# Result transposes one score later, narrow scores in turns with value products, and a later wait for the low weights, in a sparse-attention and SSM trunk

## What is computed

```python
def compressed_attention(q, kc, vc, scale): ...   # softmax over 63 compressed keys
def selected_attention(q, ks, vs, idx, scale): ... # top-16 of 16 blocks: all causal keys
def window_attention(q, kw, vw, scale):            # causal, the last 512 keys
    ...
        sc = jnp.einsum('bghtd,bsgd->bghts', qi, kk) * scale
        p = jax.nn.softmax(jnp.where(valid, sc, MASK_VALUE), axis=-1)
        return jnp.einsum('bghts,bsgd->bghtd', p, vv)
o_attn = g3[..., 0:1] * o_cmp + g3[..., 1:2] * o_slc + g3[..., 2:3] * o_win
```

## Time and profile before

| | |
|---|---|
| median of 3 executions | 937.76 us (937.34 to 938.78) |
| the profiled execution | 937.52 us |
| its span | 935.7 us |
| mean granted TensorE clock | 0.999 |
| PE busy | 896.5 us (96%) |
| VectorE, ScalarE, GpSimd busy | 520.3, 394.9, 215.0 us |
| chain that ended last, by engine | PE 88%, ACT 4%, DVE 3%, DMA 2% |

### The profile page before, as it was taken

One profiled execution on the slowest core, in us unless ns is written; L12 is line 12 of the kernel. 1 busy time (PEld: TensorE's weight loads), 2 busy tenths in 40 slices (PEclk: granted clock), 3 DMA queues, 4 the chain that ended last, 5 costly groups with the idle time before them and its releaser, 6 DMA issues.

```text
span 935.7 us, 14442 instructions
## 1 busy us (share of the span) xinstructions
PE 896.5 (96%) x5585; PEld 739.4 (79%) x5593; DVE 520.3 (56%) x1090; ACT 394.9 (42%) x793; POOL 215.0 (23%) x213
## 2 busy tenths in 40 slices
PE   2799999999999999999999999999999999999997
PEld 2478999789999777777777776788888888887885
DVE  3652273369665497797797796732223122237454
ACT  6742232522223467767768768621111111133221
POOL 3369812111002102212212212245551000000000
PEclk9999999999999999999999999999999999999999
DMA  9946042041010000000000001333232111133222
GB/s 300 338 161 92 7 114 69 1 95 46 1 47 2 1 1 1 2 1 1 2 1 1 1 1 35 79 103 95 74 96 60 48 46 44 53 128 136 90 90 90
DMA packets 61156, 59.69 MB, mean 64 GB/s; under 512 B 10240, under 2 KB 53824, under 8 KB 61072
## 3 DMA queue, kind: packets, MB, share of 16 engines
q1 hardware_dynamic: 58832, 54.13, 20.1%
q0 software_dynamic: 2000, 4.54, 1.8%
q10 hardware_dynamic: 256, 0.09, 0.0%
HBM read 52.92 MB, written 5.24 MB: 62 GB/s over the span
## 4 chain that ended last, share of the span: by engine, by line
PE 88%; ACT 4%; DVE 3%; DMA 2%; POOL 1%; issue 1%; SPq 0%; DVEq 0%; another core or an unknown queue 0%; POOLq 0%; ACTq 0%
PE bank L1723 41%; PE win_max L1723 24%; PE slc_max L1723 20%; PE bank L1726 4%; DMA xs<-in_x 1%; POOL cld L648 1%; DVE mx L1518 1%; ACT phi L846 1%; DMA cld<-in_c_im 1%; DVE mx L1525 1%; ACT pt L846 0%; ACT q L846 0%; ACT yt L846 0%; ACT osb L846 0%; SPq L518 0%
## 5 line engine op out<-in xcount | busy, mean ns | idle before, releaser
L1207 DVE TENSOR_TENSOR plo<-pt,phi 128x512 fp32r<-128x512 f32 x192 | 110.1, 590 | 42.1 <-ACT phi L846 41.7
L846 ACT ACTIVATE pt<-bank 128x512 f32<-128x512 f32 (+1 forms) x208 | 100.3, 482 | 64.0 <-PE bank L1723 61.0
L1723 PE MATMUL bank<-q,k 128*128 128x512 f32 (+7 forms) x384 | 102.6, 348 | 1.6 <-ACT phi L846 1.4
L846 ACT ACTIVATE phi<-bank 128x512 fp32r<-128x512 f32 (+1 forms) x208 | 100.3, 482 | 0.0
L1723 PEld LDWEIGHTS bank<-q,k 128*128 128x128 f32 (+1 forms) x384 | 62.6, 190 | 12.6 <-ACT phi L846 4.2
L630 POOL TENSOR_TENSOR qa<-qa,otmp 128x256 f32<-128x256 f32 x32 | 26.2, 820 | 201.7 <-DVE otmp L1207 201.7
L1518 DVE TENSOR_REDUCE mx<-slc_max 128x1 f32<-128x128 f32 (+3 forms) x64 | 48.2, 752 | 11.7 <-PE slc_max L1723 9.7
L1723 PE MATMUL bank<-ht_lo,dhi 128*128 128x512 f32 x128 | 49.8, 389 | 0.0
L1723 PE MATMUL bank<-ht_hi,dlo 128*128 128x512 f32 x128 | 49.8, 389 | 0.0
L1723 PE MATMUL bank<-ht_hi,dhi 128*128 128x512 f32 x128 | 49.8, 389 | 0.0
L1723 PE MATMUL bank<-phi,vhi 128*65 128x512 f32 (+3 forms) x128 | 45.9, 359 | 1.1 <-ACT osb L846 0.9
(11 more groups left out here) (440 smaller groups left out, 2591.9 us busy)
## 6 DMA issues: line engine op xcount, KB each, us to landing
ada<-in_w_ada SPq DMA_DIRECT2D x16, 512.0 KB, 10.3
draw<-in_w_in SPq DMA_DIRECT2D x16, 512.0 KB, 4.0
wraw<-in_w_in SPq DMA_DIRECT2D x7, 1024.0 KB, 5.3
xs<-in_x SPq DMA_DIRECT2D x8, 512.0 KB, 8.5
gstage<-in_w_ada POOLq DMA_DIRECT2D x16, 256.0 KB, 3.0
oraw<-in_w_out SPq DMA_DIRECT2D x8, 512.0 KB, 6.6
xr<-in_x SPq DMA_DIRECT2D x8, 512.0 KB, 4.4
out<-yr SPq DMA_DIRECT2D x7, 512.0 KB, 2.9
```

What stands on the lines that cost most here:

```text
L846: return nc.scalar.activation(o, i, fn, **kw)
L1207: return V.tensor_tensor(o, a, b, op)
L1723: return T.matmul(o, l, r, start=start, stop=stop, **kw)
```

## The change

Three things are done.

1. N(n) moves from behind unit u's V to behind unit u+1's S (and MX, MW), ahead of its V. Parts 0 and 1 go with it; parts 2 and 3 move one unit on, from an odd unit ahead of MX to the even unit behind it (r5, r0, r1, r2), from 19 to 20 (r3) and from 23 to 24 (r4).
2. For units 19 and 25, S and V are issued in turns: first score product, first value product, the rest of the score, the rest of the values (V is then that of units 16 and 22).
3. V of the selected and window branches waits for `exp` ahead of its first product and for `plo` only ahead of its third.

```diff
+IN_TURNS = (19, 25)
...
-    for e in range(total + LAG + 4):
+    for e in range(total + LAG + 5):
...
-        due = [n for t, n in pending if t == e - 1]
+        due = [n for t, n in pending if t == e - 2]
         maxima = more and 3 <= u < 3 + 2 * ST and u % 2 == 1
         if maxima:
             i = (u - 3) // 2
             plan += [("ND", n, part) for n in due for part in (2, 3)]
             plan += [("MX", h + 1, i), ("MW", h + 1, i)]
+        norm = [n for t, n in pending if t == e - 1]
+        plan += [("N", n) for n in norm]
         v = e - LAG
         if 0 <= v < total:
             plan.append(("V", v))
...
-        norm = [n for t, n in pending if t == e]
-        plan += [("N", n) for n in norm]
-
         parts = [[("ND", n, 0), ("ND", n, 1)] for n in norm]
         parts += [[("ND", n, 2), ("ND", n, 3)] for n in due if not maxima]
...
+                    v = vhi[br - 1][:, j, g, 0:HD + 1]
+                    mm(out_t(HD + 1), v, w, is_first, False)
+                    yield
+                    mm(out_t(HD), vlo[br - 1][:, j, g, :], w, False, False)
+                    pe.wait_ge(once("plo"), (NU - 2) * h + u - 1)
+                    ins = mm(out_t(HD + 1), v, plo[e % NPT][:, 0:hi_ - lo], False, is_last)
...
+                elif step[0] == "S" and step[1] % NU in IN_TURNS:
+                    parts = (scores(step[1]), values(step[1] - LAG))
+                    for _ in range(2):
+                        for part in parts:
+                            next(part)
```

More of the change, by code:

```diff
@@ L201, in attention_plan @@
     plan.insert(plan.index(("V", total - LAG)) + 1, ("SD",))
-    assert pending[-1][0] + 1 < total + LAG + 4 and len(pending) == 6 * HEADS
+    assert pending[-1][0] + 2 < total + LAG + 5 and len(pending) == 6 * HEADS
     b7_after, n = {}, 0
@@ L2013, in _, with scores @@
             q2_ready = [0, 0]
+            def scores(e):
+                h, u = divmod(e, NU)
+                g = h // HPG
+                br, cc, j, lo, hi_, dg, bd = units[u]
+                if u < 2:
+                    pe.wait_ge(once("b7"), q2_ready[u])
+                if e == 1:
+                    pe.wait_ge(s_eva, read_count(reads_a, len(unit_list)))
+                if e >= 2:
+                    pe.wait_ge(once("exp"), 2 * (e - 1))
+                n = hi_ - lo
+                o = bank[e % 2][:, 0:n]
+                ks = slice(P * j, P * j + P)
+                mm(o, K1(br, g, ks), q1[h % 2][:, lo:hi_], True, False)
+                yield
+                ins = mm(o, K2(br, g, ks), q2[h % 2][0:NQ2, lo:hi_], False, not (dg or bd or br == 0))
+                if br == 0:
+                    ins = mm(o, identb[:, :], cmpt[:, lo:hi_], False, True)
+                if dg:
+                    ins = mm(o[:, 0:P], maskb[:, 0, :], identb[:, :], False, not bd)
+                if bd:
+                    ins = mm(o[:, n - P:n], maskb[:, 1, :], identb[:, :], False, True)
+                ins.then_inc(once("score"), 1)
+                yield
@@ new lines, in values @@
+            def values(e):
+                h, u = divmod(e, NU)
+                g = h // HPG
+                br, cc, j, lo, hi_, dg, bd = units[u]
+                is_first = u == 0 or units[u - 1][0:2] != (br, cc)
+                is_last = u == NU - 1 or units[u + 1][0:2] != (br, cc)
+                n = 6 * h + 2 * br + cc
+                r = 2 * br + cc
+                if is_first and r == 1 and h == 0:
+                    pe.wait_ge(once("msr"), ST)
+                elif is_first and r == 5 and h + 1 < HEADS:
+                    pe.wait_ge(once("msr"), ST * (h + 2))
+                elif is_first and r in (3, 4):
+                    pe.wait_ge(once("osb"), n)
+                elif is_first and n >= 2:
+                    pe.wait_ge(once("osb"), n - 1)
+                if br == 0:
+                    pe.wait_ge(once("plo_cmp"), 2 * h + u + 1)
+                else:
+                    pe.wait_ge(once("exp"), 2 * e + 2)
+                out_t = lambda rows: acc_bank(n)[0:rows, lo - HALF * cc:hi_ - HALF * cc]
+                w = phi[e % NPT][:, 0:hi_ - lo]
+                if br == 0:
+                    mm(out_t(HD + 1), vchi[:, g, 0:HD + 1], w, True, False)
+                    yield
+                    ins = mm(out_t(HD + 1), vclo[:, g, 0:HD + 1], w, False, True)
+                else:
+                    v = vhi[br - 1][:, j, g, 0:HD + 1]
+                    mm(out_t(HD + 1), v, w, is_first, False)
+                    yield
+                    mm(out_t(HD), vlo[br - 1][:, j, g, :], w, False, False)
+                    pe.wait_ge(once("plo"), (NU - 2) * h + u - 1)
+                    ins = mm(out_t(HD + 1), v, plo[e % NPT][:, 0:hi_ - lo], False, is_last)
+                ins.then_inc(once("pv"), 1)
+                yield
@@ L2093, in attention_step @@
                     q2_ready[hf] = b7
-                elif step[0] == "S":
[L2095 to L2116, removed]
-                elif step[0] == "V":
[L2118 to L2148, removed]
@@ new lines, in attention_step @@
+                elif step[0] == "S" and step[1] % NU in IN_TURNS:
[3 more added lines that the diff above has]
+                            next(part)
+                elif step[0] == "S":
+                    for _ in scores(step[1]):
+                        pass
+                elif step[0] == "V" and step[1] + LAG < HEADS * NU and (step[1] + LAG) % NU in IN_TURNS:
+                    pass
+                elif step[0] == "V":
+                    for _ in values(step[1]):
+                        pass
```

## The result

The changed kernel takes 945.09 us (median of 4 runs, 944.75 to 946.16); the kernel before, run beside it, 937.6 (937.34 to 938.78). The ratio is 1.0077, 95% interval 1.0064 to 1.009. The profiled execution took 944.75 with a span of 942.9 and a granted clock of 0.999, so the two profiles differ by 7.2 us at the same clock.

A forecast was written before the change was run, and what follows sets the result against it. TensorE, busy 96% of the span, was taken as the bound. Six heads at +0.8 (4.9), the first +0.26 and the last -0.15 sum to +5.0: profiled 937.5 becomes 942.5, median 942.8; range 936.5 to 948.0.

The forecast's parts named there:

- Step 1: Units 5 and 6: N(r5) loses its cover, standing between maxima tile 1 and V(2); V(2) moves from 431.99 to 432.24.
- Step 2: VectorE: the `qa` write for r0 moves behind larger pieces; `plo` 6 runs beside GpSimd's sum, ending near 435.75, alone 0.59.
- Steps 3 and 4: Bank 7 is free only at 438.2; N(r1) waits until 438.35 and V(6) starts 0.94 late.
- The rest of the head: Behind V(6): units 14 to 18 come 0.70 later; MM 1 waits for bank 7 until 424.4, 0.1 later than before.
- tile 5's wait: TensorE's wait for VectorE's reductions at maxima tile 5 shrinks by some 0.2, reductions 3 and 4 coming ahead of parts 2 and 3.
- (a): Weight loads around each moved N: 0.04 gained for r5, r0, r2, 0.02 for the others, at most 0.09 each.
- (b): S and V in turns: 0.08 gained at unit 25, about 0.04 at unit 19.
- (c): N(r4) behind S(23) no longer waits for ScalarE's copy of the queries: 0.21 idle by the row, some 0.36 against N elsewhere.
- The first head: The first head has no r5 before it and no GpSimd sum: V(6) 0.4 late, +0.26.
- the share of GpSimd's CAST: Rival, chance 0.2: PQ's CAST ahead of r3's sum blocks `plo` 19 and `wrow`; 0.5 later in seven heads, +3.5, 946.3.
- (d): Later wait for `plo`: nothing gained within a head, about 0.25 once in the last three units.
- Everything stays covered: Rival, chance 0.13: r0's write delayed under 1.6, so neither N(r1) nor MM 1 waits for bank 7; about -3, 935.

## Why the prediction was right, and where it was not

The forecast was 942.8 us, range 936.5 to 948.0, slower with a chance of 0.75; it is 945.09.

- **Step 1** (V(2) 0.25 later): 0.23. Right.
- **Step 2** (`plo` 6 beside GpSimd's sum, about 1.0): 0.97. Right, and it was a full block: the sum ended at 438.18 and `plo` 6 at 438.73, 0.55 later, near the 0.59 of one alone. The rule of the Trainium skill, "SBUF — State Buffer", "Who interferes with whom", that whoever comes first holds the shared pair for its whole instruction, agrees with this row and with `wrow`, 0.57 beside the CAST.
- **Steps 3 and 4** (N(r1) behind an idle stretch, V(6) +0.94): +0.89. Right. The experiments share it out: r5's place 0.40, where my terms make it 0.55 (0.25 and 0.30), r0's 0.44, where what they leave is 0.39. So the sum came out closer than its parts, which is luck.
- **The rest of the head.** What follows tile 5's wait was to be 0.70 late. V(10) is 0.60 late (448.18 after the change, 444.56 before), S(18) 0.58. The step from 0.89 to 0.60 is 0.22 at tile 5 and 0.07 of gain (a) for r2. MM 1 was to wait for `otmp` of r4 and to swallow gains (b) and (c): it does, 0.25. Between MM 0 and MM 1 it is 4.40 (459.22 to 463.62), 4.45 before the change. With the CAST moved, S(18) to MM 1 is 8.18 against 8.11, +0.07, where the forecast had +0.11. The forecast had MM 0 in time, though, and MM 0 is 0.13 late by r3's own move.
- **The first head** (+0.26): +0.27 with the CAST out of the way, +0.65 with it.
- **What failed: the share of GpSimd's CAST.** It was the rival with a chance of 0.2, priced at 0.5 in seven heads, and it happened. I left it a rival because no row showed a CAST beside such pieces and the two starts were 0.1 apart on my clock. By the rows the CAST starts 0.2 ahead of `wrow`. It costs 0.40 a head in six heads, 2.2 between the two profiled spans and 2.6 between the medians. The rival's +3.5 was too much, by 0.1 in each head and by one head: PQ is not there in the seventh (no head after the next), whose period is +0.86. With the CAST moved a steady head is +0.72, where the forecast had +0.8, and the kernel takes 942.47, where it had 942.8.
- **Gains.** (d) was to give 0.25 in the tail. It did give 0.28 up to the transposes of `qa`, but a wait for VectorE's `dlo` stood behind them and took most of it; in the changed kernel nothing is left (31.88 against 31.86). (b) gave 0.04 to 0.05 of 0.08 at unit 25 and made ScalarE later at unit 19, where 0.04 was to be gained: together nothing. (a) is real and was put too low: from the last product of V(3) to S(8), around N(r0), it is 1.80 after the change and 1.86 before (medians of five heads), and 0.07 less around N(r2); 0.04 was given to each. (c) is real only with r4's four parts together, 0.16 a head. The tile-5 wait, a term of 0.20, measures 0.22.
- **Everything stays covered** needed `qa` to be written less than 1.6 later. It ended at 435.82 and ends at 438.16 now, on the clock of before: 2.34 later, forecast 2.4.

## What to carry to other kernels

Where a buffer is handed round, a step put later on the fast engine delays its release by all that the slower engine has queued in between; work out the release time on that engine before counting what the cover saves. Choose by instance: of six equal-looking moves one gained (r2), one gained when its tail was kept together (r4), one did nothing (r1), and two lost (r5, r0). The sixth (r3), which no run moves alone, made MM 0 0.13 late, harmless until the CAST came ahead of it as well. When a step slips by half a microsecond, look at what the third engine starts at that moment, since a small piece can be held for the whole of a large one.

## What the runs showed that was not expected

A 128x4 `wrow` takes 0.57 beside a CAST of 0.75, against 0.15 alone. How long it is held depends on the other instruction and not on its own size. It goes both ways. GpSimd's product with `zs` starts at 438.26, while `plo` 6 runs until 438.73, takes 1.07 and ends 0.60 behind it. Before the change it started first, at 434.01, and took 0.73; there `plo` 6 was the one held.

TensorE's mean granted clock differs between executions of one kernel: the kernel before had one of 940.05 us at 0.994 and one of 937.47 us at 0.999. The profiles, one for each kernel, show a fall at one place or none. ScalarE loads a table for 1.28 us there and TensorE is idle for about 1.4 of 4 us, in all 14 profiles; in six of them the clock fell. Busy time, clock (the third last number) and DMA of 320 to 324 and 324 to 328 us, in the kernel with the late wait alone:

```profile
320.00:324.00 4.00, 2.58 (x14) 1.42 (x13) 0.00 (x0) 3.99 (x7) 1.35 (x2) 1.00 0.00 0
324.00:328.00 4.00, 4.00 (x25) 3.31 (x24) 2.37 (x7) 3.49 (x10) 1.21 (x1) 0.59 0.02 4
```

and in the kernel before:

```profile
320.00:324.00 4.00, 2.58 (x17) 1.61 (x15) 0.00 (x0) 3.99 (x8) 1.61 (x2) 1.00 0.00 0
324.00:328.00 4.00, 4.00 (x28) 2.97 (x28) 3.22 (x10) 3.23 (x11) 0.94 (x1) 1.00 0.02 4
```

The activity ahead is the same, 2.58 us, and yet one falls to the lower level, 1.2 GHz, for most of the next 4 us. The first head then takes 1.2 us more (36.66 against 35.44, at a period of 35.19 in both); the six profiles are those of the table whose first head is over 1.0 longer than a steady one. Those 1.2 us are larger than several of the effects looked for. They may be most of the spread of the times of one kernel (937.24 to 939.32 here), but this is not shown. The period of a later head is free of them, which is why the table gives both.
